# Both score blocks ahead of the transposes in the differential heads' steps

## The chip, the cores and the metric

The kernel runs on one core of a Trainium2 chip. The metric is device time in microseconds (us), the median of the runs. A core has a matmul engine (TensorE, PE in the profile), three engines for elementwise work (VectorE or DVE, ScalarE or ACT, GpSimd or POOL) and a queue that issues DMAs (SyncE, SP). Each engine works through its own list of instructions in order, and they meet through semaphores.

## The reference, cut to what matters

One transformer block over 1024 tokens of width 1024, all in float32: a norm, one input projection, two kinds of attention heads beside each other, an output projection, a four-chunk MLP, a gated embedding and a last norm. The change touches the second kind of head, the differential attention of 4 heads:

```python
def one_block(args):                      # 128 queries, block bi of 8
    s = jnp.einsum('bqhtd,bkhtd->bhtqk', qb, k).astype(jnp.float32) / math.sqrt(HEAD_DIM)
    s = s + bias[None, :, None]
    s = jnp.where(mask[None, None, None], s, -jnp.inf)      # causal by chunks of 64
    pr = jax.nn.softmax(s, axis=-1)
    a = pr[:, :, 0] - lam * pr[:, :, 1]   # two softmaxes of one head, t = 0 and 1
    o = jnp.einsum('bhqk,bkhe->bqhe', a.astype(v.dtype), v)
    return (rmsnorm(o, subln_g) * (1.0 - lam_init)).astype(v.dtype)
```

## The kernel before, in words

The time goes in order through the input projections, the sliding-window heads, the four differential heads (from about 313 to 457 us of the span), and then output projection, MLP and gate, in which TensorE runs weight blocks (`wblock`, `passes`, L787) with hardly a gap.

A differential head hh has 8 units k = 0..7, one per block of 128 queries, taken in the order `ORDER = (0, 7, 1, 6, 2, 5, 3, 4)`. A unit of query block q has q + 1 key blocks of 128 (called blocks below), so the units k = 0..7 have 1, 8, 2, 7, 3, 6, 4, 5 blocks. `ROUNDS` is 2 for units of more than four blocks, which are the odd k. One unit goes through these pieces:

- S(k,t), t = 0 and 1: the two score blocks, TensorE, `score_b` L956, matmul at L970. S(k+2,t) waits until ScalarE has read S(k,t) out of the same PSUM banks (`a_e`).
- soft(k,t): VectorE adds the bias to the last 256 columns (L1353) and takes the negated maximum of the row (L1356), `soft_b` L1345.
- exp(k,t): ScalarE, `exp_b` L622, at L627. It waits for the maximum.
- mix(k): VectorE, `mix_b` L1358: reciprocal (L1366), coefficient (L1368), and the mixing of the two exponentials (L1373). It waits for exp(k,1).
- T(k,0) and, for the odd k, T(k,1): transposes of up to four blocks each, TensorE, `trans_b` L974, at L980. T(k,0) waits for mix(k). Both write PSUM bank 6, so T(k,1) waits until ScalarE has copied T(k,0) out of it.
- evac(k,r): that copy, ScalarE, `evac_b` L630, at L636.
- PV(k): attention times values, TensorE, `pv_b` L983, at L990. It waits for the last evac of its unit and for take(k-1).
- take(k): ScalarE scales the result and squares it, `take_b` L638, at L643 and L646.

The order is written out by hand, one function `step_b` for each engine. A step k of TensorE (L1003) runs S(k+2,0), T(k,0), S(k+2,1), T(k,1) if there is one, and PV(k-1). ScalarE's step k (L655) runs evac(k,0), exp(k+1,1), evac(k,1), take(k-1), exp(k+2,0). VectorE's step k (L1397) runs soft(k+1,1), soft(k+2,0), mix(k+1). Units 6 and 7 look ahead to units 0 and 1 of the next head.

From the second head on, the steps 1 to 4 also finish the head before: VectorE takes the mean (step 1) and norms its outputs (`head_norm` L1382, step 2); in steps 3 and 4 TensorE transposes one half (`out_b` L995, at L999) after T(k,0), ScalarE writes the high part (`head_hi` L649, at L652) after evac(k,0), VectorE the low part (`head_lo` L1389, at L1393) after soft(k+1,1), and TensorE waits for that low part before PV(k-1), since both use PSUM bank 7.

Steps 0 to 4 of head 0 are written out, then a hardware loop of three passes runs steps 5, 6, 7 of head hh and steps 0 to 4 of head hh + 1, and steps 5, 6, 7 of head 3 follow; of these only step 5 has scores ahead. GpSimd copies the queries of a unit into place (`stage_b` L431) once the scores four units before it are done. In head 0, ScalarE (`split_hi`, L551) and GpSimd (`split_lo`, L366) also prepare two weight blocks of the output projection.

Of the kernel before, what the change touches and what calls it, by code (L numbers as in the profile page):

```python
# [79 lines left out]
def build(nc, x, p, attn_norm_g, w_in, rel_bias, sinks, lam_q1, lam_k1, lam_q2, lam_k2, subln_g, w_out,  # L80
          mlp_norm_g, w_up, w_down, ple_norm_g, w_gate, w_ple, final_norm_g, onehot, out):
    ctx = ExitStack()
    with ctx:
# [92 lines left out]
        def e_at(k, t):  # L176

            return T + t * T if k % 2 else t * HALF

        def s_at(k, t):  # L180

            return (2 + 2 * t) * 512 if k % 2 else t * 512
# [597 lines left out]
        def _(pe):  # L780
# [175 lines left out]
            def score_b(hh, k, t):  # L956

                u = TT * hh + k
                n = (ORDER[k] + 1) * P
                pe.wait_ge(qs_ok, AU + 2 * u + t + 1)  # L960
                if isinstance(hh, int) and hh == 0 and k < 2:
                    pe.wait_ge(a_e, 2 * TT - 1 + k)
                    if k:
                        pe.wait_ge(a_at, 2 * TT)
                else:
                    pe.wait_ge(a_e, AU + 2 * (u - 2) + t + 1)
                for c in range(0, n, HALF):
                    w = min(HALF, n - c)
                    q0, s0 = (4 * t + k % 4) * P, s_at(k, t) + c
                    mm = nc.tensor.matmul(ps[:, s0:s0 + w], qs[:, q0:q0 + P],  # L970
                                          qkv[:, bass.ds((KB + hh) * T + c, w)], start=True, stop=True)
                mm.then_inc(a_s, 1)

            def trans_b(hh, k, r):  # L974

                pe.wait_ge(b_a, TT * hh + k + 1)
                pe.wait_ge(a_at, AU + HEAD_ROUNDS * hh + BEFORE[k] + r)
                for n in range(4 * r, min(4 * r + 4, ORDER[k] + 1)):
                    o, e = 6 * 512 + (n - 4 * r) * P, e_at(k, 0) + n * P
                    mm = nc.tensor.transpose(ps[:, o:o + P], e_buf[:, e:e + P], ident[:, :])  # L980
                mm.then_inc(b_t, 1)

            def pv_b(hh, k):  # L983
                u = TT * hh + k
                pe.wait_ge(a_at, AU + HEAD_ROUNDS * hh + BEFORE[k] + ROUNDS[k])
                if not (isinstance(hh, int) and u == 0):
                    pe.wait_ge(b_oc, u)
                for n in range(ORDER[k] + 1):
                    a = (k % 2) * HALF + n * P
                    mm = nc.tensor.matmul(ps[:, 7 * 512:7 * 512 + P], at_buf[:, a:a + P],  # L990
                                          qkv[:, bass.ds((VB + hh) * T + n * P, P)], start=(n == 0),
                                          stop=(n == ORDER[k]))
                mm.then_inc(b_o, 1)

            def out_b(hh, r, bank_=7):  # L995

                pe.wait_ge(b_on, hh + 1)
                for n in range(4):
                    mm = nc.tensor.transpose(ps[:, bank_ * 512 + n * P:bank_ * 512 + (n + 1) * P],  # L999
                                             o_n[:, (4 * r + n) * P:(4 * r + n + 1) * P], ident[:, :])  # L1000
                mm.then_inc(b_x, 1)

            def step_b(hh, k, ahead=True, prev=None):  # L1003
                h2, k2 = (hh, k + 2) if k < 6 else (hh + 1, k - 6)
                if ahead:
                    score_b(h2, k2, 0)
                trans_b(hh, k, 0)
                if prev is not None and k >= 3:
                    pe.wait_ge(b_oc, TT * hh + k - 1)
                    out_b(prev, k - 3)  # L1010
                if ahead:
                    score_b(h2, k2, 1)
                if ROUNDS[k] == 2:
                    trans_b(hh, k, 1)
                if prev is not None and k >= 3:
                    pe.wait_ge(a_u_ok, TT + 2 * prev + k - 2)
                if k or prev is not None:
                    pv_b(*((hh, k - 1) if k else (prev, TT - 1)))
# [21 lines left out]
            for k in range(SPLIT):  # L1040
                step_b(0, k)
            with pe.Fori(0, B_HEADS - 1) as hh:
                for k in range(SPLIT, TT):
                    step_b(hh, k)
                for k in range(SPLIT):
                    step_b(hh + 1, k, prev=hh)
# [541 lines left out]
```

## Time and profile before

| | us |
|---|---|
| median of 3 runs | 1383.09 |
| lowest, highest | 1382.09, 1386.27 |
| span of the profiled execution | 1379.7 |
| PE busy | 1333.9 |
| PE matmul spans at L970, L980 and L990 together | 136.2 |
| DVE busy | 442.2 |
| ACT busy | 355.9 |

The profiled execution's span is from its first to its last instruction; the median of the runs is 3.4 us above it, which holds what lies ahead of the first and behind the last instruction. A PE span of a group of matmuls is modelled and ends some tenths of a us behind the start of the next one, so on TensorE start-to-start times are read, not ends. In the chain of waits, a piece is the part of the end-to-end time that can be laid to that instruction.

### The profile page before, as it was taken

The numbers are of one execution on the slowest core, as the hardware profiler recorded it, in microseconds if no ns is written. First come the engines' busy times: TensorE is split into PE (matmuls) and PEld (weight loads), VectorE is DVE, ScalarE is ACT, GpSimd is POOL, SyncE is SP. The second block draws the span as 40 slices with busy tenths as digits, with TensorE's granted clock in tenths as the row PEclk, the third lists the DMA queues.
The fourth block names the chain that finished last, engine by engine and source line by source line (L and its number), as shares of the span: only waits on it lengthen the run. The fifth ranks groups of instructions, "written<-read, shape, count | busy, mean of one in ns | idle before, by whom it ended". The sixth has DMA issues, their size and how long they took to land.

```text
span 1379.7 us, 17463 instructions
## 1 busy us (share of the span) xinstructions
PE 1333.9 (97%) x6285; PEld 1090.7 (79%) x6285; DVE 442.2 (32%) x598; ACT 355.9 (26%) x655; POOL 477.8 (35%) x293
## 2 busy tenths in 40 slices
PE   6999999998888899999999999999999999999997
PEld 5788888995555788888888888888888888888886
DVE  5510112887888232222111221122211122222324
ACT  7112101665666311121011110011100122113221
POOL 3121231112221377433223432234322334774743
PEclk9999999999999999999999999999999999999999
DMA  5433111001000312111111121111121111113203
GB/s 190 173 94 92 46 46 31 0 1 31 1 0 0 138 46 60 32 59 47 46 46 46 47 60 46 46 46 46 46 60 46 46 46 46 48 43 98 70 0 123
DMA packets 117872, 75.38 MB, mean 55 GB/s; under 512 B 12817, under 2 KB 115250, under 8 KB 117458
## 3 DMA queue, kind: packets, MB, share of 16 engines
q1 hardware_dynamic: 117554, 73.93, 17.3%
q10 hardware_dynamic: 288, 1.05, 0.2%
q8 instruction: 19, 0.31, 0.1%
q14 instruction: 11, 0.09, 0.0%
HBM read 64.22 MB, written 10.75 MB: 54 GB/s over the span
## 4 chain that ended last, share of the span: by engine, by line
PE 90%; DVE 3%; ACT 2%; issue 2%; DMA 0%; DVEq 0%; SPq 0%; ACTq 0%
PE ps L787 77%; PE ps L812 3%; PE ps L903 2%; PE ps L928 2%; PE ps L970 2%; ACT e_buf L627 1%; PE ps L990 1%; PE ps L980 1%; PE ps L916 1%; DVE e_buf L1373 1%; PE ps L871 1%; DMA x_raw<-in_x 0%; PE ps L820 0%; PE ps L1072 0%; DVE coef L1368 0%
## 5 line engine op out<-in xcount | busy, mean ns | idle before, releaser
L366 POOL TENSOR_TENSOR w_lo<-w_raw,w_hi 128x1024 fp32r<-128x1024 f32 x96 | 230.9, 2406 | 621.7 <-ACT w_hi L551 621.6
L787 PE MATMUL ps<-u_hi,w_hi 128*128 128x512 f32 x896 | 277.0, 390 | 0.0
L787 PE MATMUL ps<-u_lo,w_hi 128*128 128x512 f32 x896 | 276.1, 389 | 0.0
L787 PE MATMUL ps<-u_hi,w_lo 128*128 128x512 f32 x896 | 275.8, 389 | 0.0
L551 ACT CAST w_hi<-w_raw 128x1024 fp32r<-128x1024 f32 x98 | 103.3, 1054 | 651.9 <-PE ps L787 651.1
L787 PEld LDWEIGHTS ps<-u_hi,w_lo 128*128 128x128 f32 x896 | 168.2, 188 | 35.1
L787 PEld LDWEIGHTS ps<-u_lo,w_hi 128*128 128x128 f32 x896 | 168.2, 188 | 35.1
L787 PEld LDWEIGHTS ps<-u_hi,w_hi 128*128 128x128 f32 x896 | 167.4, 188 | 35.7 <-issue 1.6
L787 PE MATMUL ps<-z_hi,w_hi 128*128 128x512 f32 x624 | 193.4, 391 | 0.0
L787 PE MATMUL ps<-z_hi,w_lo 128*128 128x512 f32 x624 | 192.1, 389 | 0.0
L787 PE MATMUL ps<-z_lo,w_hi 128*128 128x512 f32 x624 | 192.1, 389 | 0.0
L1441 DVE TENSOR_TENSOR h<-ps,h 128x1024 f32 (+1 forms) x40 | 49.0, 1225 | 306.0 <-PE ps L787 306.0
L787 PEld LDWEIGHTS ps<-z_hi,w_hi 128*128 128x128 f32 x624 | 116.8, 188 | 25.3 <-issue 1.0
L787 PEld LDWEIGHTS ps<-z_lo,w_hi 128*128 128x128 f32 x624 | 117.1, 188 | 24.4
L787 PEld LDWEIGHTS ps<-z_hi,w_lo 128*128 128x128 f32 x624 | 117.1, 188 | 24.4
L1479 DVE TENSOR_TENSOR u_lo<-temp,u_hi 128x1024 f32 x32 | 39.2, 1226 | 173.2 <-ACT u_hi L703 170.0
L1476 DVE SCALAR_TENSOR_TENSOR temp<-ps,rstd 128x1024 f32<-128x1024 f32 x32 | 39.2, 1224 | 110.1 <-PE ps L787 106.5
L970 PE MATMUL ps<-qkv,qs 128*128 (+4 forms) x192 | 73.2, 494 | 0.0
L1246 DVE SCALAR_TENSOR_TENSOR qkv<-ps,rstd 128x1024 f32 (+1 forms) x18 | 22.0, 1225 | 152.9 <-PE ps L787 146.2
L703 ACT CAST u_hi<-temp 128x1024 f32 (+1 forms) x31 | 32.5, 1049 | 138.0 <-POOL temp L498 138.0
L473 POOL TENSOR_TENSOR sqt<-h 128x1024 f32 (+1 forms) x23 | 59.3, 2580 | 17.0 <-DVE h L1508 17.0
L498 POOL TENSOR_TENSOR temp<-temp 128x1024 f32<-128x1024 f32 x32 | 60.6, 1893 | 6.0 <-DVE temp L1476 6.0
(149 smaller groups left out, 1227.8 us busy)
## 6 DMA issues: line engine op xcount, KB each, us to landing
w_raw<-in_w_up SPq DMA_DIRECT2D x64, 256.0 KB, 3.0
w_raw<-in_w_down SPq DMA_DIRECT2D x64, 256.0 KB, 3.0
w_raw<-in_w_in SPq DMA_DIRECT2D x36, 256.0 KB, 3.2
x_raw<-in_x SPq DMA_DIRECT2D x8, 512.0 KB, 6.9
h_save<-h SPq DMA_DIRECT2D x1, 4096.0 KB, 11.1
w_raw<-in_w_out SPq DMA_DIRECT2D x16, 256.0 KB, 2.9
w_raw<-in_w_ple_gate SPq DMA_DIRECT2D x16, 256.0 KB, 3.0
out<-y_out SPq DMA_DIRECT2D x6, 512.0 KB, 5.1
```

Source lines behind the costliest of these rows:

```text
L366: nc.gpsimd.tensor_tensor(w_lo[:, s * D:(s + 1) * D], w_raw[:, s * D:(s + 1) * D], w_hi[:, s * D:(s + 1) * D].bitcast(F32), ALU.subtract). ...
L473: nc.gpsimd.tensor_tensor(sqt[:, :], hj, hj, ALU.mult).then_inc(sq_t, 1)
L498: nc.gpsimd.tensor_tensor(tj, tj, tj, ALU.mult).then_inc(z_sq, 1)
L551: nc.scalar.copy(w_hi[:, s * D:(s + 1) * D], w_raw[:, s * D:(s + 1) * D]).then_inc(hi_done, 1)
L703: nc.scalar.copy(u_hi[:, bass.ds((2 * i + s) * T, T)], temp[:, s * T:(s + 1) * T]).then_inc(z_hid, 1)
L787: mm = nc.tensor.matmul(o[i], w, xx[:, x0[i]], start=(first and n == 0), stop=(last and n == 2))
L812: mm = nc.tensor.matmul(bank(2 * s + half), w, xx[:, x0], start=(k == 0 and n == 0), stop=(k == DT - 1 and n == 2))
L903: mm = nc.tensor.matmul(ps[:, g * T + j * 256:g * T + (j + 1) * 256], qs[:, (4 * g + j) * P:(4 * g + j + 1) * P], qkv[:, bass.ds(KA * T + ...
L970: mm = nc.tensor.matmul(ps[:, s0:s0 + w], qs[:, q0:q0 + P], qkv[:, bass.ds((KB + hh) * T + c, w)], start=True, stop=True)
L1441: nc.vector.tensor_tensor(hj, bank(2 * s, 2), hj, ALU.add).then_inc(ps_free, 1)
L1476: nc.vector.scalar_tensor_tensor(out=tj, in0=bank(2 * s, 2), scalar=0.0, in1=rstd[:, :], op0=ALU.max, op1=ALU.mult).then_inc(ps_free, 1)
L1479: nc.vector.tensor_tensor(u_lo[:, bass.ds(j * T, T)], tj, u_hi[:, bass.ds(j * T, T)].bitcast(F32), ALU.subtract).then_inc(z_ok, 1)
```

## The change

In TensorE's `step_b` the second score block of the unit two ahead is moved from behind the first transposes (and, in steps 3 and 4, behind the transposes of the finished head) to right behind the first score block. Nothing is added or taken away, and the other engines' lists stay as they are. The step becomes S(k+2,0), S(k+2,1), T(k,0), T(k,1) if there is one, PV(k-1).

```diff
@@ -1004,12 +1004,11 @@
                 h2, k2 = (hh, k + 2) if k < 6 else (hh + 1, k - 6)
                 if ahead:
                     score_b(h2, k2, 0)
+                    score_b(h2, k2, 1)
                 trans_b(hh, k, 0)
                 if prev is not None and k >= 3:
                     pe.wait_ge(b_oc, TT * hh + k - 1)
                     out_b(prev, k - 3)
-                if ahead:
-                    score_b(h2, k2, 1)
                 if ROUNDS[k] == 2:
                     trans_b(hh, k, 1)
                 if prev is not None and k >= 3:
```

## Rows read from the trace of the kernel before

**Rows 1.** The page: span, and the chain that ended last by engine.
```profile
span 1379.7 us, 17463 instructions
...
PE 90%; DVE 3%; ACT 2%; issue 2%; DMA 0%; DVEq 0%; SPq 0%; ACTq 0%
```
**Rows 2.** Windows, one loop pass: length, then busy us (x instructions) by engine, clock.
```profile
344.50:379.65 35.15, 30.24 (x166) 20.39 (x166) 29.45 (x61) 24.03 (x72) 7.57 (x17) 1.00 0.00 1
```
**Rows 3.** Chain of waits, 374 to 414 us: start, length, engine, line.
```profile
380.99 1.72 PE ps L970 x4
382.71 0.47 PE ps L980 x4
383.17 1.72 PE ps L970 x4
384.89 0.11 PE ps L980
...
389.67 1.30 DVE e_buf L1373
...
391.08 0.65 PE ps L980 x4
391.74 1.50 PE ps L970 x4
393.24 0.45 PE ps L980 x4
...
407.00 0.76 DVE u_lo L1393
407.81 1.83 PE ps L990 x14
...
411.67 0.79 ACT e_buf L627 x2
```
**Rows 4.** Timeline, steps 5 and 6: start, length, engine, line [idle before <-releaser].
```profile
375.41 0.60 PE L980 MATMUL ps<-ident,e_buf 128*128 128x128 f32 x4
...
375.85 1.25 PE L970 MATMUL ps<-qkv,qs 128*128 x4
...
376.05 0.58 ACT L636 COPY at_buf<-ps 128x512 f32<-128x512 f32 x1
...
376.53 0.69 ACT L627 ACTIVATE e_buf<-ps,nmax 128x512 f32<-128x512 f32 x1
...
376.93 0.38 PE L980 MATMUL ps<-ident,e_buf 128*128 128x128 f32 x2
...
377.43 0.17 DVE L1366 RECIPROCAL rden<-den_t 128x2 f32<-128x2 f32 x1
...
378.77 0.65 PE L980 MATMUL ps<-ident,e_buf 128*128 128x128 f32 x4 [0.57 <-DVE e_buf L1373]
```
**Rows 5.** Timeline, step 7 of the last head, which has no scores ahead.
```profile
452.38 0.66 PE L980 MATMUL ps<-ident,e_buf 128*128 128x128 f32 x4 [1.59 <-DVE e_buf L1373]
...
453.81 0.30 PE L980 MATMUL ps<-ident,e_buf 128*128 128x128 f32 x1 [0.77 <-ACT at_buf L636]
```
**Rows 6.** Timeline, step 2 of a later head: maximum and exponential of unit 3.
```profile
394.52 1.09 DVE L1356 TENSOR_REDUCE nmax<-ps 128x1 f32<-128x896 f32 x1
...
396.03 1.04 ACT L627 ACTIVATE e_buf<-ps,nmax 128x896 f32<-128x896 f32 x1
```
**Rows 7.** Timeline, head 0, steps 2 to 5.
```profile
330.76 0.94 DVE L1368 SCALAR_TENSOR_TENSOR coef<-rden,den_t,nlam 128x1 f32<-128x1 f32 x1
...
336.69 1.02 PE L970 MATMUL ps<-qkv,qs 128*128 128x512 f32 x2
...
337.55 1.72 PE L990 MATMUL ps<-qkv,at_buf 128*128 128x128 f32 x14
...
340.20 0.65 PE L980 MATMUL ps<-ident,e_buf 128*128 128x128 f32 x4
```
**Rows 8.** Windows of PE alone: length, busy us, granted clock, DMA share.
```profile
313.00:316.00 3.00, 3.00 (x7) 0.58 0.00 0
```

## The prediction

> **What bounds the kernel now.** I read the page first, then the windows, then the chain of waits inside the heads, and last the timeline beside it. The page lays 90% of the chain to PE [rows 1]: outside the heads TensorE is the bound, so what the heads gain or lose goes one to one into the span. The windows show that inside the heads it isn't so simple. One pass of the loop takes 35.15 us, and PE is busy 30.24, DVE 29.45 and ACT 24.03 of it at full clock [rows 2]. No engine is full; a loop of waits between the three sets the pass. So I follow the chain through one pass and ask at each step whether S(k+2,1), the block that moves, lies on it, and what the chain does when the block is ahead of T(k,0).
>
> The chain runs: exp(6,1), mix(6), T(6), S(0,1) of the next head, PV(5), S(1,0), T(7,0), S(1,1), T(7,1), PV(6), take(6), exp(1,0), exp(1,1), mix(1), T(1,0), S(3,1), T(1,1), evac(1,1), exp(3,1), mix(3), the norm of the finished head, its two transposes with head_hi and head_lo, PV(3), S(7,0), T(5,0), evac(5,0), and exp(6,1) again [rows 3]. The last link is the one to note: ScalarE's list puts evac(k,0) ahead of exp(k+1,1). A late T(k,0) therefore makes exp(k+1,1) late, and with it mix(k+1), though neither needs the transposes.
>
> **The change, step by step.** The instructions are the same before and after, and so is their busy time; only positions count. Two costs come in. First, T(k,0) can't start before S(k+2,1) is through. Second, nothing stands any more between T(k,0) and T(k,1), so TensorE waits there for evac(k,0) to free bank 6. The trace has that very case in step 7 of the last head: from T(7,0) to T(7,1) it takes 453.81 - 452.38 = 1.43 us [rows 5]. There T(7,0) came after an idle time. When it follows a matmul without a gap, evac starts 0.64 behind it [rows 4], which is a little sooner, so I take 1.40. In the other direction, wherever TensorE sits idle ahead of T(k,0), waiting for mix(k), S(k+2,1) fills the hole for nothing.
>
> Step 5: there is no idle time ahead of T(5,0); it starts right behind S(7,0). S(7,1) takes 376.93 - 375.85 = 1.08, so T(5,0) goes from 375.41 to 376.49. evac(5,0) began 0.64 behind T(5,0) and exp(6,1) 0.48 behind that, and the reciprocal of mix(6) began 0.12 behind the end of the exponential [rows 4], so nothing absorbs it. Cost **+1.08**. Before, S(7,1) lay beside the evacuation and off the chain.
>
> Step 6: TensorE waits 0.57 for mix(6) [rows 4]. S(0,1) is one block, an eighth of the 1.72 of eight blocks [rows 3], 0.22, and slips into the wait. PV(5) moves up by that. **-0.22**.
>
> Step 7: S(1,1) was on the chain between T(7,0) and T(7,1) and stays on it, now ahead of T(7,0). From T(7,0) to T(7,1) it took 384.89 - 382.71 = 2.18. Now it is 1.72 ahead of T(7,0) and 1.40 behind it. 1.72 + 1.40 - 2.18 = **+0.94**. T(7,0) itself becomes 2.6 us late (1.08 - 0.22 + 1.72), and exp of unit 0 with it, but mix(1) doesn't hang on that; it hangs on PV(6), take(6) and the exponentials of unit 1, which come 1.80 late.
>
> Step 0: one round of transposes and a block of 0.43; PV(7) waits for take(6) anyway. Zero.
>
> Step 1: mix(1) ends at 389.67 + 1.30, and T(1,0) starts at 391.08 after an idle time [rows 3]. S(3,1) takes 1.50. It may begin once exp(1,1) has been read, which is the event that also starts mix(1), and mix(1) needs 0.46 for reciprocal and coefficient and 1.30 for the mixing; so it just fits. Then T(1,1) follows T(1,0) by 1.40, where it was 393.24 - 391.08 = 2.16 [rows 3]: a gain of 0.76 on TensorE's side. But exp(3,1) also needs its maximum from VectorE, which has worked without a gap since mix(1). The maximum ended at 394.52 + 1.09 = 395.61 and the exponential began at 396.03 [rows 6]. With 0.04 for the signal, only **-0.38** of the gain gets through.
>
> Steps 2, 3 and 4: mix(3), the norm, the transposes of the finished head, head_hi and head_lo now follow the maximum of unit 3. T(3,0) gets later by the 1.29 of S(5,1), but it had more than that in hand: the transposes of the finished head wait for the norm anyway, and behind them evac(3,0) is through, so T(3,1) has no new wait. PV(2) and PV(3) wait for head_lo as before: head_lo ran from 407.00 to 407.76 and PV(3) started at 407.81 [rows 3]. What is saved by having S(6,1) out of the way is lost in that wait. Zero.
>
> One pass: 1.08 - 0.22 + 0.94 - 0.38 = **+1.42**.
>
> The first pass is milder. In head 0 no finished head holds PV(3); it started as soon as S(6,1), 337.55 - 336.69 = 0.86 long, had gone through [rows 7]. With S(6,1) ahead of T(4), in the time of mix(4), PV(3) and S(7,0) come 0.86 sooner, and the 1.08 of S(7,1) makes T(5,0), 340.20 before, only 0.2 late. So 0.2 - 0.22 + 0.94 - 0.38 = +0.54. Behind the loop, step 5 of head 3 costs its 1.08 again, of which 0.07 vanish in small waits, and steps 6 and 7 have no scores: +1.01.
>
> Sum: 0.54 + 2 x 1.42 + 1.01 = 4.39; the timeline's finer spacings of head 0 take a tenth off, and I take **+4.3 us**. The profiled execution would go from a span of 1379.7 to 1384.0, and with the 3.4 us around it the median from 1383.09 to 1387.4.
>
> In head 0, GpSimd's weight split can start sooner, since the staging ahead of it does. A coefficient of VectorE took 0.94 there against 0.22 elsewhere, and ended with such a split [rows 7]. This can move 0.7 us from one mix to another; both have slack of about that size, so I count none and keep 0.7 each way. The Trainium skill, "SBUF — State Buffer", section "Who interferes with whom", says that a VectorE instruction with two SBUF inputs and a GpSimd instruction that reads SBUF exclude each other for a whole instruction; the 0.94 agrees. It gives no other sum.
>
> Bounds. Lowest: step 5 is covered in every pass as in the first, 3 x 0.54 + 0.2 = 1.8, less the 0.7. Highest: nothing comes back at steps 1 and 6, 1.08 + 0.94 = 2.0 a pass, 7.2 with the last step, plus a little.
>
> **Rivals.** *The holes win (faster).* If exp(k+1,1) were bound by its maximum and not by evac(k,0), steps 5 and 7 would cost nothing, and the blocks would go into the waits ahead of T(1,0) and T(6): (0.22 + 0.76) x 3 = 2.9 us gained, 1380.2. It decides at the point where VectorE's maximum comes later than evac(k,0) ends. For it: PE idles there, 0.57 us ahead of T(6) [rows 4] and longer ahead of T(1,0). Against it: exp(6,1) starts on the tail of evac(5,0), and the chain itself goes through that copy [rows 3, 4]. Chance 0.04.
>
> *Step 5 is covered (small loss).* If PV(3) came sooner in later heads too, the sum is 1.8 and the time 1384.9. Against it: head_lo releases PV(3) [rows 3]. With what lies between it and my sum, 0.25.
>
> *Nothing comes back (larger loss).* S(3,1) doesn't fit ahead of T(1,0), or waits signal later than I read: 5.5 to 7.2 more, about 1389.6. Chance 0.15.
>
> *The clock falls.* From 313 to 316 us the granted clock was 0.58, most of it at the 1.2 GHz level, after waits of TensorE at the end of the window heads [rows 8]. New waits of about 0.9 us in the odd steps could bring such a stretch into each later head: 3 us at half speed, 1.5 us of work lost three times, on top of 4.3: 1391.9. Against it: the pass with its present idle time of 5 us stands at 1.00 [rows 2]. Chance 0.03. The Trainium skill, "TensorE: Matmul & The Clock Gate", section "HAM oscillation — how this bites in real kernels", warns that gaps ahead of each group of matmuls can throttle the engine again and again; by that rule it would be the 1391.9, and the trace so far speaks against it.
>
> **How the numbers follow.** My forecast has 0.53 (3.2 to 5.5 us slower). 0.3% is 4.15 us, about what a measurement of this kernel can tell from no change, and the forecast lies on that line. Of its 0.53 I put 0.31 above and 0.22 below; with 0.18 of the two larger losses, slower is 0.49, same 0.22 + 0.25 = 0.47, faster 0.04. Range 1384.3 to 1390.2.
>
> **What would show it.** In the profile after: T(k,0) to T(k,1) 1.4 us apart in steps 1, 5 and 7, with idle time released by at_buf; T(5,0) 2.16 behind S(7,0); exp(6,1) still on the tail of evac(5,0); no idle time ahead of T(1,0); 36.6 us a pass for the second and third, about 35.7 for the first. I am wrong if exp(6,1) starts ahead of evac(5,0)'s end, if the passes stay at 35.15, or if the clock leaves 1.00.

## The result and the profile after

The changed kernel takes 1389.36 us in the median of 6 runs (1384.44 to 1390.61), the kernel before 1382.51 in runs beside it: a ratio of 1.0039 with a 95% interval of 1.0023 to 1.0054, slower by 3 to 7.5 us. The span of its profiled execution is 1386.0, 6.3 above before's 1379.7 [rows 1]; with 3.1 us around it, that execution took 1389.12.

The page, its span and the chain by engine:

```profile
span 1386.0 us, 17463 instructions
...
PE 91%; DVE 3%; ACT 2%; issue 2%; DMA 1%; SPq 0%; DVEq 0%; ACTq 0%
```

One pass of the loop from PV(3) to PV(3) took 35.11, 35.15 and 35.04 us before, and 36.34, 36.43 and 37.96 now. The windows of the second pass, from S(7,0) to S(7,0), with the columns of rows 2:

```profile
373.55:409.99 36.44, 30.56 (x167) 20.93 (x166) 29.52 (x61) 23.87 (x70) 7.70 (x17) 1.00 0.00 0
```

The work is the same (DVE 29.5, ACT 23.9) and the clock is full; 1.3 us more of waiting is all that differs from [rows 2]. The timeline of steps 5 and 6 in that pass, the rows that answer to [rows 4]:

```profile
375.72 0.60 PE L980 MATMUL ps<-ident,e_buf 128*128 128x128 f32 x4
...
376.36 0.59 ACT L636 COPY at_buf<-ps 128x512 f32<-128x512 f32 x1 [1.12 <-PE ps L980]
376.84 0.69 ACT L627 ACTIVATE e_buf<-ps,nmax 128x512 f32<-128x512 f32 x1
376.99 0.44 PE L980 MATMUL ps<-ident,e_buf 128*128 128x128 f32 x2 [0.68 <-ACT at_buf L636]
...
377.74 0.17 DVE L1365 RECIPROCAL rden<-den_t 128x2 f32<-128x2 f32 x1 [1.19 <-ACT e_buf L627]
...
379.08 0.65 PE L980 MATMUL ps<-ident,e_buf 128*128 128x128 f32 x4 [0.50 <-DVE e_buf L1372]
```

The exponential (L627) still stands on the tail of the evacuation (L636), 0.48 behind its start, and the reciprocal, which had come without a wait before, now has 1.19 us of idle VectorE ahead of it. The steps 7 and 1 that follow, the transposes of TensorE (answering to the chain pieces of [rows 3]):

```profile
384.34 0.60 PE L980 MATMUL ps<-ident,e_buf 128*128 128x128 f32 x4
...
385.62 0.33 PE L980 MATMUL ps<-ident,e_buf 128*128 128x128 f32 x1 [0.68 <-ACT at_buf L636]
...
392.04 0.65 PE L980 MATMUL ps<-ident,e_buf 128*128 128x128 f32 x4
...
393.37 0.66 PE L980 MATMUL ps<-ident,e_buf 128*128 128x128 f32 x4 [0.68 <-ACT at_buf L636]
```

T(7,1) follows T(7,0) by 1.28 us and has a wait for the copy ahead of it. T(1,0) at 392.04 has no idle time ahead of it any more: S(3,1) fills the hole exactly.

And what I had priced as a rival only, the granted clock. Windows of TensorE alone, first before, with the columns of [rows 8]:

```profile
438.00:440.00 2.00, 1.27 (x6) 1.00 0.00 0
440.00:442.00 2.00, 1.84 (x9) 1.00 0.00 0
...
460.00:462.00 2.00, 2.00 (x11) 1.00 0.00 0
462.00:464.00 2.00, 2.00 (x11) 1.00 0.00 0
```

and after:

```profile
438.00:440.00 2.00, 0.61 (x6) 1.00 0.00 0
440.00:442.00 2.00, 2.00 (x6) 0.53 0.00 0
...
460.00:462.00 2.00, 1.46 (x7) 0.65 0.86 332
462.00:464.00 2.00, 2.00 (x8) 0.50 0.90 381
```

TensorE drops to the 1.2 GHz level twice, for 3.4 us each. The first is at step 4 of head 3, where it makes the third pass 1.6 us longer (37.96 - 36.43, and before's third pass is 0.11 shorter than its second). The second is behind the last head, between T(7,1) and the transposes that stand in the first output block. Before (T(7,1) itself is in [rows 5]):

```profile
463.99 1.03 PE L999 MATMUL ps<-ident,o_n 128*128 128x128 f32 x8
```

and after:

```profile
458.23 0.30 PE L980 MATMUL ps<-ident,e_buf 128*128 128x128 f32 x1 [0.77 <-ACT at_buf L636]
...
470.22 1.03 PE L999 MATMUL ps<-ident,o_n 128*128 128x128 f32 x8
```

That is 11.99 us against 10.18, 1.8 more, of which 0.15 is a later start of PV(6) ahead of the drop. Before had one such drop, at the start of the heads [rows 8], and after hadn't, which gives 1.1 us back. So of the 6.3 us between the two profiled executions 3.9 come from the order of the work (head 0 and first pass +0.36, second and third +1.3 each, behind the loop +0.99) and 1.6 + 1.7 - 1.1 = 2.2 from the clock.

### The profile page after: what moved, and what is told of

It is laid out like the page before. It is cut to its first block, busy times and chain, and to the rows that moved or that the text cites. A ratio compares the mean times of both kernels' runs of the same rounds, so it can differ in the third digit from the quotient of the medians.

```text
span 1386.0 us, 17463 instructions
## 1 busy us (share of the span) xinstructions
PE 1340.2 (97%) x6285; PEld 1095.7 (79%) x6285; DVE 443.3 (32%) x598; ACT 356.0 (26%) x655; POOL 478.7 (35%) x293
## 4 chain that ended last, share of the span: by engine, by line
PE 91%; DVE 3%; ACT 2%; issue 2%; DMA 1%; SPq 0%; DVEq 0%; ACTq 0%
PE ps L787 76%; PE ps L812 3%; PE ps L970 2%; PE ps L903 2%; PE ps L928 2%; PE ps L990 1%; ACT e_buf L627 1%; PE ps L916 1%; PE ps L980 1%; PE ps L871 1%; DMA x_raw<-in_x 1%; DVE nmax L1355 1%; ACT at_buf L636 0%; DVE e_buf L1372 0%; PE ps L837 0%
## 5 line engine op out<-in xcount | busy, mean ns | idle before, releaser
L970 PE MATMUL ps<-qkv,qs 128*128 (+4 forms) x192 | 69.4, 497 | 0.9 <-ACT e_buf L627 0.9
```

What stands on the lines that cost most here:

```text
L970: mm = nc.tensor.matmul(ps[:, s0:s0 + w], qs[:, q0:q0 + P], qkv[:, bass.ds((KB + hh) * T + c, w)], start=True, stop=True)
```

## The experiments

Each kernel ran 5 to 12 times unless said otherwise, in three groups, and every group had runs of before beside it, with medians of 1382.84, 1382.01 and 1382.29. Kernels of different groups are therefore compared by their ratios to before, not by their times. "Pass" is the time from PV(3) to PV(3) of the next head with the clock at 1.00.

**The changed kernel again** (no edit). Three theories from here on. "Order": the loss is what the moved blocks do to the chain of waits. "Every new wait counts": each new wait between two transposes costs its own length. "Clock": part of the loss is time at the 1.2 GHz level.

> The changed kernel once more, as the comparison for the others on this chip. Theory 'order': the moved block costs 3.9 to 4.3 us by position alone (1.3 to 1.4 in each of the later passes, 0.4 in the first, 1.0 behind the loop), the same in every run; what a run has beyond that is stretches at half clock. Rival 'every new wait counts': TensorE's wait between the two transposes of a unit costs its own 0.7 us in all 15 odd steps, about 10 us. Order expects a median 4 to 6 us above before, with passes of 36.4 us wherever the clock stays at 1.00.

Measured: 1389.43 us, ratio 1.0043 (1.0028 to 1.0058), passes of 36.32 and 36.42. Its profiled execution, 1391.84, had drops of the clock at 409, at 447 and behind the last head for 7 us. The passes are as order has them; the median is above what order alone gives.

**Only steps 5 and 7.**

```diff
+                first = k in (5, 7)
                 if ahead:
                     score_b(h2, k2, 0)
+                    if first:
+                        score_b(h2, k2, 1)
                 trans_b(hh, k, 0)
...
-                if ahead:
+                if ahead and not first:
                     score_b(h2, k2, 1)
```

> The block ahead of the transposes in steps 5 and 7 alone; before's order in the others. Order: these two steps hold the whole loss, and the gains of steps 1 and 6 are missing, so a pass costs 1.08 + 0.94 = 2.0 us: 3 passes and the last step 5, 6.5 to 7.1 us slower than before, more than the whole change. Rival 'every new wait counts': 7 of the 15 waits remain, so it should cost about half of what the whole change does, 2 to 3 us.

Measured: 1388.07 us, ratio 1.0036 (1.0022 to 1.0050), passes of 36.99, 37.08 and 37.00. The three PV(3) in question, each with a wait of 0.92 for head_lo, as before has it:

```profile
374.97 1.83 PE L990 MATMUL ps<-qkv,at_buf 128*128 x14 [0.92 <-DVE u_lo L1396]
...
412.05 1.83 PE L990 MATMUL ps<-qkv,at_buf 128*128 x14 [0.92 <-DVE u_lo L1396]
...
449.05 1.72 PE L990 MATMUL ps<-qkv,at_buf 128*128 x13 [0.92 <-DVE u_lo L1396]
```

(449.05 - 374.97) / 2 = 37.04, against 35.10 before: +1.94 a pass, where 2.0 was expected. Two of the eight moves of a pass cost more than all eight. "Every new wait counts" is out: it had these two steps at half the loss. The median missed, though: it is 5.2 us above before's, where 6.5 to 7.1 was expected, and below the repeat's 1389.43. The mean clock of these runs is 0.9935, against 0.9921 in before's runs beside them and 0.9912 in the repeat of the changed kernel, so these runs lost less to the clock than either; what that is worth is worked out behind the list of the prediction's steps.

**All but steps 5 and 7** (`first = k not in (5, 7)`).

> The block ahead of the transposes in all steps but 5 and 7. Order: only the gains are left, 0.22 at step 6 and 0.38 at step 1 of each pass, and 0.6 at step 1 of head 0, of which about 0.3 gets through: 1.8 to 2.4 us faster than before, passes of 34.5 us. Rival 'every new wait counts': the waits of steps 1 and 3 remain, so slower than before by 2 to 5 us.

Measured: 1381.55 us, ratio 0.9989 (0.9979 to 0.9998): faster than before, though TensorE's waits between the two transposes of step 1 are there (in step 3 only head 0 has one, since in the later heads the finished head's transposes stand between the two). The pass is 34.68, 0.47 less than 35.15. The gain, 1.3 us by the medians, is under the 1.8 to 2.4 us expected; its profiled execution fell to half clock from 406 to 410.

**ScalarE's order turned round in step 5.**

```diff
+                if k == 5:
+                    exp_b(h1, k1, 1)
                 evac_b(hh, k, 0)
                 if prev is not None and k >= 3:
                     head_hi(prev, k - 3)
-                if ahead or k < 7:
+                if (ahead or k < 7) and k != 5:
                     exp_b(h1, k1, 1)
```

> The changed kernel with ScalarE's list turned round in step 5: exp(6,1) ahead of evac(5,0). If the loss of step 5 comes through ScalarE's order (a late transpose makes the next exponential late), mix(6) is on time again; what is left is PV(4), 0.95 late, of which about 0.2 reaches PV(5). So 0.8 to 0.9 of the 1.08 goes, in three passes and less behind the loop (there take(4) still comes late, so 0.3 to 1): 2.5 to 3.5 us below the changed kernel. If instead TensorE's own late start of T(5,0) and PV(4) makes the loss, within 0.5 us of the changed kernel.

Measured: 1387.92 us, ratio 1.0033 (1.0019 to 1.0047), and a pass of 408.19 - 372.08 = 36.11, 0.3 below the changed kernel's and not 0.8 to 0.9. The median is 1.5 below the repeat's, not 2.5 to 3.5. This expectation missed, and its rival (within 0.5) did too. The trace shows why. With exp(6,1) on time, the next thing that is late is PV(5):

```profile
379.37 0.79 PE L992 MATMUL ps<-qkv,at_buf 128*128 x5 [0.17 <-ACT o_sq L646]
```

It waits for take(4), which waits for PV(4), for T(5,1), for evac(5,0), for T(5,0). From S(7,0) to PV(5) it is 5.15 us before, 6.02 in the changed kernel and 5.63 here. The late T(5,0) thus runs on two routes, by ScalarE's order to exp(6,1) and by TensorE's own to PV(4); opening the first is worth 0.39 of the 0.87, then the second holds.

**Useless matmuls in the waits of steps 6 and 7 of the last head** of the changed kernel ("the fill"), to see what the clock behind it is worth.

```diff
+                last = isinstance(hh, int) and hh == B_HEADS - 1
+                def extra(n):
+                    nc.tensor.matmul(ps[:, 0:n], qs[:, 3 * P:4 * P],
+                                     qkv[:, (KB + hh) * T:(KB + hh) * T + n], start=True, stop=True)
...
+                if last and k == 7:
+                    extra(HALF // 2)
                 if ROUNDS[k] == 2:
                     trans_b(hh, k, 1)
...
                     pv_b(*((hh, k - 1) if k else (prev, TT - 1)))
+                if last and k == 6:
+                    extra(HALF)
+                    extra(HALF // 2)
+                if last and k == 7:
+                    extra(3 * P)
```

> The changed kernel, with matmuls of no use in TensorE's waits of steps 6 and 7 of the last head (768, 256 and 384 columns of queries times keys, to banks that nothing reads), each a little shorter than the wait it stands in. Theory 'clock': part of the change's loss is that TensorE, with longer holes, falls to half clock behind the last head, which cost 1.8 us in the profiled execution of the changed kernel. Then the stretch from 456 to 468 us stays at 1.00 and the median is 1 to 3 us below the changed kernel's 1389.4. Rival 'order alone': the median is the changed kernel's within 0.5 us, since nothing on the chain of waits moves.

Measured: 1388.10 us, ratio 1.0040 (1.0025 to 1.0055). The clock behind the heads stays full, as the windows of this kernel show, but it fell at 404 to 408 instead:

```profile
400.00:420.00 20.00, 15.49 (x85) 0.91 0.00 0
...
456.00:468.00 12.00, 11.21 (x57) 1.00 0.37 132
```

The median is 1.3 below the changed kernel's 1389.4, but by the ratio to before (1.0040 against 1.0039 and 1.0043) nothing is gained: by its time this run is inconclusive. A cost of the fill that its expectation didn't have is told at "before with the useless matmuls" below.

**Before's order in steps 3 and 4** of the changed kernel (`k not in (3, 4)`).

> The changed kernel with before's order in steps 3 and 4. There the block that has gone ahead leaves holes of 1.4 and 1.8 us ahead of PV(2) and PV(3), where it was 0.2 and 0.9. Order alone: these steps cost nothing in the passes (36.4 us each), and in head 0 the 0.86 lead of PV(3) is lost, so 0.5 to 0.9 us above the changed kernel. Clock: with the holes shorter again TensorE falls to half clock less often in 400 to 455 us, each fall being 1.6 us, so the median is 1 to 2.5 us below the changed kernel in spite of that.

Measured: 1387.65 us, ratio 1.0040 (1.0026 to 1.0054), a pass of 36.42, the changed kernel's. So steps 3 and 4 cost nothing by order in the passes. In head 0 the move gains 0.3 there: from T(0,0) to PV(3) it is 17.80 us in the changed kernel and 18.12 here (316.25 to 334.37). Its profiled execution has no drop in 400 to 450 us, but one of 7 us from 455 on, and by the ratio the 1 to 2.5 us that "clock" expected to gain aren't there.

**Both of these together.**

> Both at once: before's order in steps 3 and 4 and the useless matmuls behind the last head. If clock and order are all there is, what is left is order alone: 3.9 us for the changed positions plus up to 0.9 for head 0, 1386.5 to 1387.5 with falls no more frequent than before. If the holes have nothing to do with the falls, 1389 to 1390.

Measured: 1386.37 us, ratio 1.0028 (1.0016 to 1.0039), mean clock 0.994 against 0.991 in the changed kernel's runs. That is 4.4 us above before by the medians and 3.9 by the ratio, and lies with "order alone"; it is the only one of the three whose ratio comes down, and its interval still overlaps the changed kernel's.

**The move only in steps 0, 1, 2 and 6** (`k in (0, 1, 2, 6)`), meant to beat both.

> A version to beat both: the block ahead only in steps 0, 1, 2 and 6, where TensorE waits for VectorE's mixing or nothing is lost, and between the transposes in 3, 4, 5 and 7. Order: passes of 34.7 us against 35.15, and 0.3 to 0.5 in head 0, so 1.7 to 2 us below before. With the shorter holes of steps 3 and 4 the clock falls no more often than before: 1380.5 to 1381.2, at or under the version that leaves only steps 5 and 7 alone (1381.55). If the holes don't matter, the same as that version.

Measured: 1381.85 us, ratio 0.9996 (0.9985 to 1.0007). The order is right, 440.10 - 405.40 = 34.70 us a pass, but the profiled execution spent 451 to 458 us at half clock. With the short holes of steps 3 and 4 there was no drop in the passes. What step 1 brings in this kernel:

```profile
389.12 0.65 PE L980 MATMUL ps<-ident,e_buf 128*128 128x128 f32 x4
...
390.45 0.66 PE L980 MATMUL ps<-ident,e_buf 128*128 128x128 f32 x4 [0.68 <-ACT at_buf L636]
...
392.55 1.09 DVE L1358 TENSOR_REDUCE nmax<-ps 128x1 f32<-128x896 f32 x1
...
393.68 1.01 ACT L627 ACTIVATE e_buf<-ps,nmax 128x896 f32<-128x896 f32 x1
```

The exponential of unit 3 begins 0.04 us behind its maximum (393.64), where 0.42 lay between them before [rows 6]: VectorE has become the bound there, as the prediction had it.

**The same with the useless matmuls.**

> The block ahead in steps 0, 1, 2 and 6 alone, with the useless matmuls behind the last head. Order: passes of 34.7 us and 0.3 to 0.5 in head 0, 1.7 to 1.9 us below before. Clock: without the fill this version fell to half clock from 451 to 458 us in its profiled execution and gave 1381.85 in the median; with it the stretch behind the last head stays at 1.00, so 0.5 to 1.8 us lower, 1380 to 1381.3. If the fill doesn't act on the falls, 1381.85 again.

Measured: 1380.63 us, ratio 0.9982 (0.9972 to 0.9992), the lowest of all, though its interval overlaps those of the two selective kernels without the fill, with the clock at 1.00 from 400 to 468 us. By the ratio it beats before by 1.1 to 3.9 us, and it lies 8 to 9 us under the changed kernel.

**Before with the useless matmuls.**

> Before with the useless matmuls behind its last head and nothing else: what the fill is worth, or costs, without the change. Clock: before fell there in none of what its profile shows, but its slower runs may hold such falls, so 0 to 1 us below before, and none above it. If the fill stood in the way of the chain of waits, 0.3 to 1 us above.

Measured: 1382.90 us, ratio 1.0006 (0.9995 to 1.0016). No effect on the time can be told, but the trace shows that the fill isn't free. Its last head takes no longer, and the transposes in the first output block stand where they do without it:

```profile
463.80 1.03 PE L999 MATMUL ps<-ident,o_n 128*128 128x128 f32 x8
```

Yet its span is 1380.9 us against 1379.7. From these transposes to the end of the span it takes 917.1 to 917.2 us in all four profiles with the fill and 915.7 to 915.8 in all nine without: 1.4 us, all of it at the very end, where SyncE's last six DMAs of the output land 6.2 us after their issue in the median, and 5.0 to 5.1 in the kernels without. Why four matmuls in the last head lengthen these isn't shown. Nor is it so that before's clock hardly falls: of its 23 runs beside this one, seven have a mean clock of 0.991 or less, with spans of 1381.2 to 1385.2, and nine have 0.994, with 1378.6 to 1379.5. None of the 12 runs with the fill is under 0.992. So the fill seems to buy back here about what it costs.

**Only step 5**, a single run (`k == 5`).

> The block ahead in step 5 alone, one look. It parts the 1.97 us a pass that steps 5 and 7 cost together. The prediction has 1.08 for step 5, of which S(1,0) and all behind it get the whole where step 6 gives nothing back: passes of 36.1 to 36.25 us. If step 7 carried nearly all of it (a late T(7,0), whatever step 5 does), passes of 35.2 to 35.5.

Measured: 1386.09 us and a pass of 410.28 - 374.06 = 36.22, so step 5 costs 1.07 alone, and step 7 the other 0.9 of the 1.94.

**The drops, over all profiles.** Where the block goes ahead in steps 3 and 4, PV(2) and PV(3) have 1.4 and 1.8 us of idle TensorE ahead of them, against 0.2 and 0.9. Of the five profiles with these holes (the changed kernel, its repeat, all but 5 and 7, ScalarE turned round, and the one filled at the end) four have a drop between 400 and 450 us; of the eight without, before among them, none. From 451 us on, about the last steps and behind the last head, five of nine profiles without the fill show one, and none of the four with it. Both stretches were picked after the drops had been seen, and the same two holes in the first pass (PV(2) at 366.75 and PV(3) at 371.89 in the changed kernel) are followed by a drop in none of the five. So the holes make a drop likelier; they don't decide it. The rows of before and then of the changed kernel show them:

```profile
402.66 0.71 PE L990 MATMUL ps<-qkv,at_buf 128*128 x4 [0.19 <-DVE u_lo L1393]
...
407.81 1.83 PE L990 MATMUL ps<-qkv,at_buf 128*128 x14 [0.92 <-DVE u_lo L1393]
```

```profile
403.18 0.71 PE L990 MATMUL ps<-qkv,at_buf 128*128 x4 [1.39 <-DVE u_lo L1392]
...
408.32 1.83 PE L990 MATMUL ps<-qkv,at_buf 128*128 x14 [1.78 <-DVE u_lo L1392]
```

## Why the prediction was right, and where it wasn't

It forecast 1387.4 in a range of 1384.3 to 1390.2; 1389.36 lies in it, on the slower side, where I had put 0.49. The order of the work, which the whole sum rests on, came out step by step as below. That the time itself fell into the range is in part luck: by the medians the loss is 6.9 us, above the 3.2 to 5.5 of the forecast proper, and it landed in the part of the range that I had opened for "nothing comes back", which didn't happen. My own sign of being wrong, that the clock leaves 1.00, did appear.

- Step 5, +1.08: measured 1.09 from PV(3) to T(5,0) in the changed kernel and 1.07 a pass with step 5 alone. Of its reason I named one route, ScalarE's order; the turned list showed a second, through PV(4) and take(4), that is late by nearly as much. "Nothing absorbs it" holds for both. (The 0.12 from exponential to reciprocal isn't in the rows named, which give 377.43 - (376.53 + 0.69) = 0.21; nothing hangs on it.)
- Step 6, -0.22: right where step 5 is late too (PV(5) comes 0.22 sooner against T(5,0)). With steps 5 and 7 left alone it is worth nothing, since T(7,0) then waits for mix(7), which ended at the same moment as S(1,0).
- Step 7, +0.94: measured +0.87. From T(7,0) to T(7,1) it is 1.28 us, not 1.40; the row I took it from [rows 5] stands outside the loop, where the changed kernel too has 1.37 to 1.43.
- Step 1, -0.38: measured -0.44. S(3,1) fits exactly into the hole, and the gain stops at VectorE's maximum.
- Steps 2, 3 and 4, zero: right by order for 3 and 4; the pass is 36.42 with or without them. Step 2 wasn't tried alone. What the prediction left out is what the same step does to the length of the holes.
- One pass +1.42: measured +1.3. Head 0 and first pass together: -0.86 for PV(3) of head 0 and 1.40 for the pass behind it, 0.54 net; measured -0.87 and +1.23, 0.36 net. Behind the loop +1.01: measured +0.99. The sum by order is 3.9, for 4.3.
- The faster rival fell: in steps 5 and 7 the exponential does wait for evac(k,0). Its gains exist where they are taken alone, but as 0.47 a pass (34.68 and 34.70 for 35.15) and not 0.98, because VectorE's maximum stops the one and mix(7) the other.
- The clock, 0.03 for a rival of its own: mis-sized. I asked whether the new waits of 0.9 us in the odd steps would bring drops, and by the pass at full clock called it unlikely. The drops came, but at the 1.4 and 1.8 us holes of steps 3 and 4 and behind the last head, one or two in a run instead of three. As the Trainium skill, "TensorE: Matmul & The Clock Gate", section "HAM oscillation — how this bites in real kernels", warns, gaps ahead of groups of matmuls brought the engine back to its lower clock; the trace agrees on that much, though the page's own case is longer waits, for DMAs, and here no idle time ahead of these drops was over 1.8 us.
- What the clock is worth over the runs. In the profiled executions it is 2.2 of the 6.3 us, but these are one execution each. Every run lists its span and mean clock, and a line through 155 of these runs, with one offset for each kernel and group, gives 0.85 us of span for each 0.001 of mean clock. The changed kernel's eleven runs have a mean span of 1386.8 and a mean clock of 0.9913, before's twenty beside the repeat 1381.2 and 0.9921. Of these 5.5 us only 0.7 go with the clock, and at equal clock 4.9 are left (standard error 0.4); steps 5 and 7 alone come to 6.1 in the same way, all but 5 and 7 to -1.7. This is an estimate, since the mean clock also counts drops at the ends of the program that may cost another amount. By it, order is by far the larger part of the loss, and about 1 us beyond the 3.9 of the traces stays open.

## What to carry to other kernels

Moving work ahead of a wait pays only where the engine idles at that point in the trace; look at each step of a written-out schedule by itself, since here the same move gains in one step and costs in two others, and the kernel that leaves those two alone (0.9989) was a little faster than either. Work standing between two dependent operations is cover: before taking it out, look up what the second waits for and what else is queued behind the first on the engine that serves both. And equal idle time isn't equal: if a move joins short holes of TensorE into longer ones, look at the granted clock in several profiles, not in one, and compare the mean clock of all runs before laying a difference to it.

## What the runs showed that I had not expected

- Transposes that wait for the copy of those before them follow by 1.27 to 1.33 us inside the loop and by 1.37 to 1.43 outside it (changed kernel). Idle time of TensorE ahead of the first isn't the difference: the pair at 322.37 and 323.79 has none and is 1.42 apart. What is stays open.
- In the passes and behind them the clock fell where TensorE hadn't been idle for more than 1.8 us at a time. In the changed kernel's third pass the two score blocks of unit 6 took 3.56 us instead of the 1.88 of the pass before, and nearly all of that, 1.6 us, reached the pass.
- Matmuls of no use, 1408 columns in the waits of the last head's steps 6 and 7, cost that head nothing and kept its end at full clock in four of four profiles, but all four profiles are 1.4 us longer at the end of the program. With both effects in it, the time of before didn't change (1.0006, 0.9995 to 1.0016), and the selective kernel went from 0.9996 to 0.9982, with intervals that overlap.
